# Second attention of a two-block kernel: group outputs issued in pieces, a buffer pair for each group, four mixed tiles kept in device memory

## What is computed

```python
def block(args):                       # one block of 128 queries of one head
    qi, bi = args
    s = jnp.einsum('bhqd,bhkd->bhqk', qi, kt).astype(jnp.float32) * scale
    s = jnp.where(mask[None, None], s, -1e30)
    pr = jax.nn.softmax(s, axis=-1).astype(vt.dtype)
    return jnp.einsum('bhqk,bhkd->bhqd', pr, vt)
...
return jnp.concatenate([ret_out, mla_out], axis=-1) @ w_o
```

## Time and profile before

| | us |
|---|---|
| median of 3 runs | 2279.16 (2277.14 to 2283.83) |
| the profiled execution's own time | 2278.32 |
| its span in the trace | 2276.3 |
| PE busy in the span | 2085.4 (92%) |
| DVE busy | 1167.8 (51%) |
| POOL busy | 708.5 (31%) |
| ACT busy | 703.0 (31%) |
| mean granted PE clock, of full speed | 0.957 |

### The profile page before, as it was taken

How to read it: one execution, slowest core, us unless ns; L and a number is a source line. 1 busy time by engine, 2 the same in 40 slices (tenths; PEclk the granted TensorE clock), 3 DMA queues, 4 the chain that set the end, 5 groups by cost and what they waited for, 6 DMA issues and landing times.

```text
span 2276.3 us, 24686 instructions
## 1 busy us (share of the span) xinstructions
PE 2085.4 (92%) x9915; PEld 1718.9 (76%) x9915; DVE 1167.8 (51%) x1592; ACT 703.0 (31%) x1220; POOL 708.5 (31%) x460
## 2 busy tenths in 40 slices
PE   4988998999799999978888798999999999999878
PEld 3976866777687888856776586788888888888667
DVE  5244127999677354455544446444443344444745
ACT  3011125888443223236555444200000000000541
POOL 2332305888100000005556100333343334433020
PEclk9988998999899999989998799999999999999989
DMA  3112100000333111100000222111111111111012
GB/s 136 47 38 78 38 19 1 1 1 1 111 93 131 55 38 37 39 28 19 19 19 19 93 92 65 56 54 49 47 47 48 54 47 47 47 56 65 29 37 93
DMA packets 34304, 113.42 MB, mean 50 GB/s; under 512 B 3664, under 2 KB 5456, under 8 KB 34192
## 3 DMA queue, kind: packets, MB, share of 16 engines
q1 hardware_dynamic: 24336, 88.20, 12.3%
q10 hardware_dynamic: 9856, 23.65, 2.8%
HBM read 103.46 MB, written 8.39 MB: 49 GB/s over the span
## 4 chain that ended last, share of the span: by engine, by line
PE 77%; DVE 11%; ACT 5%; POOL 4%; issue 2%; DMA 1%; ACTq 0%; SPq 0%; POOLq 0%; DVEq 0%
PE psb L316 21%; PE psa L316 20%; PE psd L316 10%; PE psc L316 9%; PE psd L909 2%; PE psd L1829 2%; PE psc L887 1%; PE psc L1792 1%; POOL pb L1046 1%; DVE wl L343 1%; PE psc L356 1%; DVE ptl L1010 1%; DVE tiny L993 1%; POOL qst L844 1%; DVE tiny L1760 1%
## 5 line engine op out<-in xcount | busy, mean ns | idle before, releaser
L327 POOL TENSOR_TENSOR wh<-wraw,one 128x1024 fp32r<-128x1024 f32 x82 | 156.4, 1907 | 756.3 <-PE psc L316 267.7
L330 POOL TENSOR_TENSOR wl<-wraw,wh 128x1024 fp32r<-128x1024 f32 x82 | 198.6, 2422 | 6.4
L316 PE MATMUL psb<-mh,wh 128*128 128x512 f32 x512 | 174.5, 397 | 2.4 <-issue 2.4
L316 PE MATMUL psa<-mh,wh 128*128 128x512 f32 x448 | 158.7, 407 | 17.2 <-ACT mh L1089 14.4
L1781 POOL TENSOR_TENSOR lps<-lps,tiny 128x128 f32<-128x128 f32 (+2 forms) x24 | 14.7, 613 | 511.2 <-DVE tiny L1776 510.6
L316 PE MATMUL psb<-ml,wh 128*128 128x512 f32 x512 | 172.6, 393 | 0.0
L316 PE MATMUL psb<-mh,wl 128*128 128x512 f32 x512 | 172.4, 392 | 0.0
L316 PE MATMUL psa<-ml,wh 128*128 128x512 f32 x448 | 156.0, 401 | 3.2 <-DVE ml L2083 2.7
L316 PE MATMUL psa<-mh,wl 128*128 128x512 f32 x448 | 154.8, 398 | 0.0
L1046 POOL TENSOR_TENSOR pb<-pb,tiny 128x1024 f32<-128x1024 f32 x64 | 121.2, 1894 | 85.8 <-DVE tiny L1004 84.1
L2132 ACT ACTIVATE th<-hf 128x1024 f32<-128x1024 f32 x22 | 23.3, 1061 | 391.4 <-DVE hf L2146 391.4
(11 more groups left out here) (528 smaller groups left out, 5079.6 us busy)
## 6 DMA issues: line engine op xcount, KB each, us to landing
wraw<-slabs SPq DMA_DIRECT2D x160, 512.0 KB, 3.5
x<-xT SPq DMA_DIRECT2D x8, 520.0 KB, 10.2
h<-xT ACTq DMA_DIRECT2D x8, 512.0 KB, 6.3
residual<-h ACTq DMA_DIRECT2D x8, 512.0 KB, 6.7
h<-residual ACTq DMA_DIRECT2D x8, 512.0 KB, 7.6
outT<-h ACTq DMA_DIRECT2D x16, 256.0 KB, 2.1
ct<-dft ACTq DMA_DIRECT2D x1, 1300.0 KB, 5.9
st<-dft ACTq DMA_DIRECT2D x1, 1300.0 KB, 8.8
```

The source lines that it names most:

```text
L316: t = e.matmul(o, lhsT=lw, rhs=xx(kt, c0, cn), start=n == 0, stop=n == total - 1, skip_group_check=True)
L327: e.tensor_tensor(WH[j][:, :], RAW[:, j, :], ONE[:, 0:1].to_broadcast([P, 1024]), MUL).then_inc(*pooled.up(("high", s)))
L330: e.tensor_tensor(WL[j][:, :], RAW[:, j, :], WH[j][:, :], SUB).then_inc(*pooled.up(("split", s)))
```

## The change

- The product of a group is cut into pieces: two for group 0 (key tiles 0 and 1; 2 and 3), three for group 1 (0 to 2; 3 to 5; 6 and 7). `out_due(U)` gives the piece that PE issues at step U, behind turns, scores and projection. Group 0 of head h, complete at U = 8h+6, is issued at U = 8h+7 and 8h+8; group 1, complete at U = 8h+10, at U = 8h+11 to 8h+13, that is in steps w = 3, 4, 5 of the next head. ("o", U) is raised by the last piece.
- ACT's L1839 and DVE's L1845 move to the step behind the last piece (w = 1 for group 0, w = 6 for group 1 of the head before). On ACT it stands behind exps, on DVE ahead of `dve_mla_parts`.
- `LTH` and `LTL` become pairs. Group 1 keeps the old places; group 0 gets 8 KB each at 140 and 148 KB, where tiles 0 to 3 of `MX` lie. The parts' wait for ("o", U-1) becomes one for ("o", U-5).
- So these four tiles are stored to device memory by one DMA ("mix kept", 2 MB) that ACT issues before the loop, and loaded back by one ("mix back") that ACT issues at U = 64, behind ("o", 59). Parts(0) wait for the store on ACT and DVE; the splits behind the attention wait for the load.
- `act_key_parts` is as it was.

```diff
-        LTH = at("lth", [P, 8, HALF], F32R, 108)
-        LTL = at("ltl", [P, 8, HALF], F32R, 27)
+        LTH = [at(f"lth{j}", [P, 4 + 4 * j, HALF], F32R, (140, 108)[j]) for j in range(2)]
+        LTL = [at(f"ltl{j}", [P, 4 + 4 * j, HALF], F32R, (148, 27)[j]) for j in range(2)]
...
+        ms = nc.dram_tensor("retained", (4, P, T), F32, kind="Internal").ap()
...
+        PIECES = (2, 3)
+
+        def out_due(U):
+
+            last = 4 * ((U - LAG - 3) // 4) + 3 if U >= LAG + 3 else -1
+            piece = U - LAG - last - 1
+            return (last, piece) if last >= 0 and 0 <= piece < PIECES[last % 8 // 4] else (last, None)
+
+        def out_done(U):
+
+            last, piece = out_due(U - 1)
+            return last if piece is not None and piece == PIECES[last % 8 // 4] - 1 else None
...
         def act_mla_parts(e, U):
             u, v = U % 8, U % 4
-            if v == 0 and U >= 4:
-                e.wait_ge(*psum.on(("o", U - 1)))
+            if U == 0:
+                e.wait_ge(*landed["mix kept"].on("all"))
+            if v == 0 and U >= 8:
+                e.wait_ge(*psum.on(("o", U - 5)))
...
-        def pe_mla_out(e, U):
+        def pe_mla_out(e, U, piece):
+
             h, u = divmod(U, 8)
             g = u // 4
             nk = 4 * g + 4
-            e.wait_ge(*vec.on(("lp low", U)))
-            e.wait_ge(*vec.on(("v2", h)))
-            if U >= 4:
-                e.wait_ge(*vec.on(("mout", U - 4)))
-            for kt in range(nk):
+            if piece == 0:
+                e.wait_ge(*vec.on(("lp low", U)))
+                e.wait_ge(*vec.on(("v2", h)))
+                if U >= 4:
+                    e.wait_ge(*vec.on(("mout", U - 4)))
+            step = 2 + g
+            for kt in range(step * piece, min(step * piece + step, nk)):
...
-            t.then_inc(*psum.up(("o", U)))
+            if piece == PIECES[g] - 1:
+                t.then_inc(*psum.up(("o", U)))
...
@@ pe_mla
-                if b >= 0 and b % 4 == 3:
-                    pe_mla_out(e, b)
+                last, piece = out_due(U)
+                if piece is not None:
+                    pe_mla_out(e, last, piece)
...
@@ act_mla
+            e.wait_ge(*vec.on(("gn out", RH - 1)))
+            load(e, "mix kept", ms.rearrange("n p t -> p n t"), MX[:, 0:4, :])
             act_split(e, S_MLA + 2)
...
                     act_mla_parts(e, b)
                 if U < NM2:
                     act_mla_exps(e, U)
+                if out_done(U) is not None:
+                    act_mla_out(e, out_done(U))
+                if U == NM2:
+                    e.wait_ge(*psum.on(("o", NM2 - 5)))
+                    e.wait_ge(*vec.on(("lp low", NM2 - 5)))
+                    load(e, "mix back", MX[:, 0:4, :], ms.rearrange("n p t -> p n t"))
                 if w < 4 and h + 1 < MH_:
                     act_mla_projected(e, h + 1, w)
-                if b >= 0 and b % 4 == 3:
-                    act_mla_out(e, b)
...
@@ dve_mla
-                if b >= 0:
+                if out_done(U) is not None:
+                    dve_mla_out(e, out_done(U))
+                if 0 <= b < NM2:
                     dve_mla_parts(e, b)
-                if b >= 0 and b % 4 == 3:
-                    dve_mla_out(e, b)
```

More of the change, by code:

```diff
@@ L260, in two_block_kernel @@
         landed = {}
-        for name in (["cols", "squares", "cos1", "sin1", "wf", "cd", "ct", "st", "pos", "rx", "pos2", "mask", "p"]
+        for name in (["cols", "squares", "cos1", "sin1", "wf", "cd", "ct", "st", "pos", "rx", "pos2", "mask", "p", "mix kept", "mix back"]
                      + [f"{n}{m}" for n in ("x", "h", "spill", "h2") for m in range(KT)]):
@@ L1803, in act_mla_parts @@
                 e.wait_ge(*psum.on(("mturned", U, b)))
-                e.activation(LTH[:, k0:k1, v * P:v * P + P],
+                e.activation(LTH[u // 4][:, k0:k1, v * P:v * P + P],
                              PS[C][:, b, 0:(k1 - k0) * P].rearrange("p (k q) -> p k q", q=P), ACT.Copy
@@ L1812, in dve_mla_parts @@
                 e.wait_ge(*acted.on(("lp high", U, b)))
-                t = e.tensor_tensor(LTL[:, k0:k1, v * P:v * P + P],
+                t = e.tensor_tensor(LTL[u // 4][:, k0:k1, v * P:v * P + P],
                                     PS[C][:, b, 0:(k1 - k0) * P].rearrange("p (k q) -> p k q", q=P),
-                                    LTH[:, k0:k1, v * P:v * P + P], SUB)
+                                    LTH[u // 4][:, k0:k1, v * P:v * P + P], SUB)
             t.then_inc(*vec.up(("lp low", U)))
-        def pe_mla_out(e, U):
+        def pe_mla_out(e, U, piece):
             h, u = divmod(U, 8)
@@ L1821, in pe_mla_out @@
             nk = 4 * g + 4
-            e.wait_ge(*vec.on(("lp low", U)))
-            e.wait_ge(*vec.on(("v2", h)))
-            if U >= 4:
-                e.wait_ge(*vec.on(("mout", U - 4)))
-            for kt in range(nk):
+            if piece == 0:
[5 more added lines that the diff above has]
+            for kt in range(step * piece, min(step * piece + step, nk)):
                 c0 = max(0, kt - 4 * g) * P
-                for hl, Pt in enumerate((LTH, LTL)):
+                for hl, Pt in enumerate((LTH[g], LTL[g])):
                     t = e.matmul(PS[Dp][:, 1, c0:HALF], lhsT=VS2[h % 2][:, kt, :], rhs=Pt[:, kt, c0:HALF],
                                  start=kt == 0 and hl == 0, stop=kt == nk - 1 and hl == 1, skip_group_check=True)
-            t.then_inc(*psum.up(("o", U)))
+            if piece == PIECES[g] - 1:
+                t.then_inc(*psum.up(("o", U)))
         def act_mla_out(e, U):
@@ L1854, in pe_mla @@
             pe_mla_scores(e, 0)
-            for U in range(NM2 + LAG):
+            for U in range(NM2 + LAG + 4):
                 b, h, w = U - LAG, U // 8, U % 8
-                if b >= 0:
+                if 0 <= b < NM2:
                     pe_mla_turns(e, b)
@@ L1975, in act_out2 @@
                 load(e, f"h2{m}", H[:, m, :], hs[m])
+            e.wait_ge(*landed["mix back"].on("all"))
             act_split_half(e, MX, 0, "mix2")
```

## The result

The changed kernel takes 2292.83 us (median of 7 runs, 2289.19 to 2294.3) where the kernel before takes 2277.14 in the same comparison: ratio 1.0064, 95% interval 1.0053 to 1.0075. It is slower by about 15 us, more than the 0.3% that a measurement can tell. The profiled execution took 2293.3 us, its span is 2291.3.

A forecast was written before the change was run, and what follows sets the result against it. PE was taken as the bound, idle 4.5 us a head, so only the order could win. The profiled 2278.32 us plus 9.0 summed over the heads gave 2287.3; with the median 0.8 above, 2288. Range 2275 to 2299.

The forecast's parts named there:

- The bound: Whole attention stretch: PE leads, idle 4.5 us a head; new buffers alone bring nothing, only the order of work can win.
- The key part's wait: ACT's key part, heads 1 to 6: waits for group 1's last piece; V starts T3 + 4.5, PE idle 2.2, before 0.40.
- Pieces of G1: Group 1's product on PE: first twelve products lengthen T1 to T3 by 2.64 us, to 4.03 and 3.04; last four 0.41.
- T4 to T5: Between turns of four and five tiles: group 0 leaves, but DVE's group 1 sum precedes low parts; 4.2 us at full clock.
- the flat 1.0 for the clock: Allowance per head for half-clock time beyond that hidden in waits: 1.0 us, between bounds of 0 and 2.5.
- about 2 as a sign: In the trace after, PE should idle about 2 us before the turns of five tiles.
- T5 to T6, T7 to T8: Turns of five to six tiles: 2.25 us. Seven to eight: group 0's sum precedes low parts, 4.64 us, PE idle 1.1.
- Clock: PE's half-clock spell expected to start at V or T4, after longer waits; 1.0 us taken, making a head 32.9.
- rival 3: Clock falls twice a head, or the store is late: 1.5 us more for six heads, 2297, or 2300 with store; 17%.
- Head 0: Hands on its group 1 product, no key wait, wins 0.7 at T6, loses 1.1 + 0.4 behind: 29.1 becomes 26.9 us.
- Heads 6 and 7: Head 6: key wait, no projections behind T6, +2.3 us. Head 7: takes group 1's pieces, loses 1.2 at T8, 28.0 becomes 28.4.
- Store and load: DMA issues on ACT's queue: both cost nothing unless late; store 0 to 3 us, taken as 0; formula 6.8 us for 2 MB.

The follow-up runs named there:

- the memory alone: The kernel before with only the changed one's memory (buffer pair for each group, store and load back), order of work old: 2278.21 us, ratio 1.0006.
- the order alone: The kernel before, single buffer pair, whole group products; ACT's group copy one step later behind exps, DVE's sum one step later behind low parts: 2258.5 us, ratio 0.9918.
- three orders: The order alone; that with S(7) ahead of T4; and that also with POOL's query part ahead of unit 5's norm: 2258.5, 2254.2 and 2255.27 us.
- the key part set free: The changed kernel, but the key part waits for the last scores that read its place instead of the last group product: 2278.05 us, ratio 1.0005.
- both repairs: The changed kernel, with the key part waiting for the last scores and DVE's group sum behind the low parts: 2259.82 us, ratio 0.9922.
- S(7) ahead of T4: The order alone, with PE issuing the scores S(7) ahead of the turns of four tiles: 2254.2 us, ratio 0.9898.

## Why the prediction was right, and where it was off

The direction and the mechanisms were right, and the measured median lies in the range; the size was under-estimated, 9.0 for a difference of 15.0 between the two profiled executions. The term that was too small is the clock: most of the missing 6 us are time at half clock.

- *The bound.* That the group buffer limits nothing is shown by the memory alone (1.0006), and that the win lies in the order by the order alone (0.9918). The Trainium skill (Perfetto Trace Analysis, Optimization Strategy) names missing SBUF or PSUM as one meaning of repeated bubbles. For SBUF the runs of this case speak against it; for PSUM the 8.3 us from V to T6 that three orders did not shorten would agree with it, but no run has a second pair C.
- *The key part's wait.* Forecast T3 to V 4.45 with 2.2 idle in heads 1 to 6; measured 4.44 with 2.21. Its price was put at 2.2 a head, 13.4 in all; taking it away gave 14.8 for six heads.
- *Pieces of G1.* Forecast T1 to T2 to T3 4.03 + 3.04; measured 3.97 + 2.69, 0.4 less than I gave them.
- *T4 to T5.* Forecast 4.2 at full clock; measured 4.79 to 4.92 in heads 1 to 6. T4 itself ran at half clock in all of these (1.09 instead of 0.63), and the chain starts at its end; I had put this into the flat 1.0 for the clock. With T4 at full clock, in the run with the key part set free, it is 4.33 to 4.45, so the chain itself was put 0.1 to 0.25 too short. PE idled 1.0 to 1.4 before T5, where I had named about 2 as a sign.
- *T5 to T6, T7 to T8.* Forecast 2.25 and 4.64; measured 2.39 in the heads at 0.95, 3.36 in heads 2 to 4, and 4.64 to 4.78. The wait before T8 came as forecast (0.96 to 1.10 in heads 0 to 5).
- *Clock.* This is the term that was mis-sized. Heads 1 and 5, at 0.95, took 32.4 us where 32.9 was forecast. Heads 2, 3 and 4, at 0.84 to 0.85, took 33.5, 33.8 and 33.9; in each of them the clock stood at half for some 10 us on end, from about V's end over T4 and T5 to T6 (in head 3 from 1144.0 to 1154.0), where the spells of heads 1 to 5 lasted 3.5 in the kernel before. This is not rival 3's two spells, but one that did not end; its price, 1.1 to 1.5 above heads 1 and 5, is near the 1.5 that the rival gave. At full clock the parts add up to the 31.9 of the forecast, as the 0.4 too much at T1 to T3 is made up by what T4 to T6 had too little. No head took the 32.9 of the forecast: that the five together come within 1.5 of it is the mean of two without the long stretch and three with it, and partly luck. My reading of the spells before was also too simple. In head 1 the spell lies at 1083.0 to 1086.5, behind the wait before T6 and not round V, and the order alone keeps both waits round V and has T4 at full clock in all heads.
- *Head 0* took 28.6 instead of 26.9. S(0) waited 2.40 for POOL's query part, which ended 5.3 behind T4 as forecast. Then the clock was at half from 1052.0 to 1055.0: G0's first piece took 1.54 instead of 0.8, so that T4 to T6 was 7.25 and not 6.45, and T6 to T7 took 4.56 instead of 3.65. That is the whole 1.7. The step that failed there is the clock in head 0, which I put at nothing, since before the change that head had 1.00.
- *Heads 6 and 7.* 32.1 and 30.6 instead of 30.9 and 28.4. In the tail the same two waits of the sum stand with nothing else to run. Head 6 has its T4 and S(7) at half clock, V to T5 8.06 us; at full clock, in the run with the key part set free, it is 7.02. In head 7 I had priced T8 at 1.2 (measured 1.6) and left out the sum's wait before T5, which made T4 to T5 4.32 instead of 3.37. The last G1 ran for 6.04 us, wholly at half clock, where before it took 4.99 and ended at full clock.
- *Store and load* cost nothing, as taken. Landing in 7.0 and 7.9 us is a little above the 6.8 that the Trainium skill's formula (DMA: Bandwidth & Descriptors, Anatomy of one DMA), which is for another issuing path, gave as an estimate.

By heads, forecast against measured: 26.9 and 28.6; 164.5 and 166.0 for heads 1 to 5; 30.9 and 32.1; 28.4 and 30.6. The differences, 1.7 + 1.5 + 1.2 + 2.2, are the 6 us that were missing and 0.5 more, which was made up outside the heads. All of the first two, most of the third and about half of the last lie where a row ran at half clock; the rest is the sum's wait in head 7. What makes the clock fall was not tested by a run of its own.

## What to carry to other kernels

When a step is made later, look for every wait that names it as a stand-in for something else: here the keys' place was guarded by a group product that had always been long done, and moving the product by three steps turned that free wait into one of 2.2 us a head. Where an engine runs a list in order, put what others need at once ahead of what nobody waits for; the sum of a group behind the low parts was worth 20 us, more than all buffers. Try the order alone before paying memory for it.

## What was unexpected of the hardware

PE's granted clock fell to 1.2 GHz at T4 in four of seven heads before the change and in heads 1 to 6 after it, although PE's longest single wait there was 1.5 us before and 2.2 us after; the two waits stand round 1.06 us of transposes. The same waits give either level: in the kernel before T4 took 0.90 in head 3 and 0.63 in head 0. The runs say more. With no wait before V in heads 1 to 6 (the key part set free, and both repairs) T4 took 0.63 in every head. In the order alone it did so too, though the waits round V are those of before (0.39 to 0.44, and 1.50); what is shorter there is the wait some 20 us ahead of the next V, 1.2 before S(0) where it was up to 2.43 before T6. So the two waits round V don't decide it alone, and which idle time does stays open.

The clock also doesn't need PE to be free of waits. With S(7) ahead of T4 it stayed at 1.00 for 191 us, with some 0.4, 1.4 and 1.2 us idle in a head (0.43, 1.41 and 1.19 in head 3).
